# First mixer with its output product in three passes over halves split on GpSimd, input weights laid out by use, areas filled in another order, constants loaded last

## What is computed

```python
def token_mixer(x, w_in, b_in, sinks, ln_v_g, ln_v_b, w_spatial, b_spatial, w_out, b_out):
    proj = x @ w_in + b_in
    q, k, v = proj[..., :o1], proj[..., o1:o2], proj[..., o2:o3]
    u, g = proj[..., o3:o4], proj[..., o4:]
    attn = sliding_window_attention(q, k, v, sinks)
    sgu = chunked_spatial_gating(u, g, ln_v_g, ln_v_b, w_spatial, b_spatial)
    return jnp.concatenate([attn, sgu], axis=-1) @ w_out + b_out

mix = token_mixer(x, ...)
h = layer_norm(DEEPNORM_ALPHA * x + mix, ln1_g, ln1_b)
ffn = routed_experts(h, ...)          # 32 experts, top 4, each 3 x 1024 x 1024 weights
x = layer_norm(DEEPNORM_ALPHA * h + ffn, ln2_g, ln2_b)
```

## Time and profile before

| | us |
|---|---|
| median of 3 runs | 1471.69 |
| lowest, highest | 1471.09, 1472.19 |
| the profiled execution | 1471.71 |
| its span, first to last instruction | 1469.9 |
| TensorE busy | 1393.4 (95%) |
| VectorE busy | 535.1 (36%) |
| ScalarE busy | 342.0 (23%) |
| GpSimd busy | 90.1 (6%) |

### The profile page before, as it was taken

The page is one execution under the profiler, slowest core; times in us unless marked ns, Lnnn a source line. Parts: engine busy times, 40 slices in busy tenths (PEclk is TensorE's granted clock), DMA queues, the critical chain, the costliest instruction groups (busy, mean ns, idle before and its releaser), DMA issues.

```text
span 1469.9 us, 23417 instructions
## 1 busy us (share of the span) xinstructions
PE 1393.4 (95%) x10106; PEld 788.4 (54%) x10106; DVE 535.1 (36%) x980; ACT 342.0 (23%) x504; POOL 90.1 (6%) x44
## 2 busy tenths in 40 slices
PE   8999999999998999899898999999999999999998
PEld 6553333333333333333333333333979989899997
DVE  1772111211211211121112111213989658777766
ACT  0531000100100110010001000102765543444442
POOL 0000000000000000000000000002000050122232
PEclk9999999999999999999999999999999999999999
DMA  9799999999999999999999999998544114255552
GB/s 363 267 401 396 428 428 428 435 432 431 428 433 433 431 430 430 431 433 430 429 426 436 432 427 434 433 427 364 181 144 144 75 44 159 89 198 185 189 182 86
DMA packets 34469, 491.36 MB, mean 334 GB/s; under 512 B 3825, under 2 KB 4337, under 8 KB 12305
## 3 DMA queue, kind: packets, MB, share of 16 engines
q1 hardware_dynamic: 34272, 490.47, 80.5%
q10 hardware_dynamic: 144, 0.13, 0.0%
HBM read 489.54 MB, written 1.05 MB: 334 GB/s over the span
## 4 chain that ended last, share of the span: by engine, by line
PE 67%; DMA 28%; DVE 2%; ACT 1%; issue 0%; POOL 0%; SPq 0%; DVEq 0%; ACTq 0%
DMA ring<-in_w_exp 18%; PE bank L891 17%; DMA work<-in_w_exp 10%; PE bank L920 9%; PE bank L948 8%; PE bank L949 8%; PE bank L950 8%; PE bank L844 2%; PE bank L832 2%; PE bank L703 2%; PE bank L755 2%; PE bank L673 1%; ACT spare L1537 1%; PE bank L852 1%; PE bank L911 1%; PE bank L906 0%
## 5 line engine op out<-in xcount | busy, mean ns | idle before, releaser
L891 PE MATMUL bank<-ring,spare 128*64 128x512 f32 x1344 | 300.6, 600 | 24.0 <-DMA ring<-in_w_exp 23.8
L2066 DVE TENSOR_SCALAR work<-bank 128x512 f32<-128x512 f32 x32 | 22.1, 691 | 739.7 <-PE bank L891 739.7
L891 PEld LDWEIGHTS bank<-ring,spare 128*64 128x64 f32 x1344 | 98.4, 138 | 214.8 <-issue 184.3
L920 PE MATMUL bank<-ring,spare 128*64 128x512 f32 x672 | 148.8, 595 | 14.7 <-ACT spare L1537 14.7
L949 PE MATMUL bank<-work_parts,ring_parts 128*128 128x256 f32 x568 | 159.4, 281 | 0.0
L1533 ACT ACTIVATE work<-work 128x512 f32<-128x512 f32 x32 | 20.2, 631 | 534.5 <-DVE work L2066 534.5
L891 PE MATMUL bank<-work,spare 128*64 128x512 f32 x576 | 128.0, 593 | 8.4 <-DMA work<-in_w_exp 8.4
L949 PEld LDWEIGHTS bank<-work_parts,ring_parts 128*128 128x128 f32 x568 | 107.8, 190 | 1.1
L920 PEld LDWEIGHTS bank<-ring,spare 128*64 128x64 f32 x672 | 46.9, 137 | 103.1 <-issue 90.3
L948 PE MATMUL bank<-hn_hi,ring_parts 128*128 128x256 f32 x352 | 99.4, 282 | 0.0
L950 PE MATMUL bank<-hn_hi,ring_parts 128*128 128x256 f32 x352 | 99.1, 282 | 0.0
(11 more groups left out here) (467 smaller groups left out, 1977.4 us busy)
## 6 DMA issues: line engine op xcount, KB each, us to landing
ring<-in_w_exp SPq DMA_DIRECT2D x57, 4096.0 KB, 31.5
work<-in_w_exp SPq DMA_DIRECT2D x17, 4096.0 KB, 31.6
work<-in_w_exp SPq DMA_DIRECT2D x20, 2048.0 KB, 28.1
spare<-in_w_exp SPq DMA_DIRECT2D x12, 2048.0 KB, 28.3
ring<-in_w_exp SPq DMA_DIRECT2D x12, 2048.0 KB, 24.3
ring<-in_ffn_up SPq DMA_DIRECT2D x22, 1024.0 KB, 4.8
ring<-in_ffn_down SPq DMA_DIRECT2D x22, 512.0 KB, 3.4
ring<-in_w_in SPq DMA_DIRECT2D x2, 2048.0 KB, 17.4
```

Of the source, the lines that this page charges most:

```text
L891: ins = pe.matmul(to[n2 * CAP:(n2 + 1) * CAP, :], x_e[:, 4 * j + 2 * half + kk, :], w[:, b, kk, n2 * BANK:(n2 + 1) * BANK], start=False, s ...
L920: ins = pe.matmul(y_bank[n2 * CAP:(n2 + 1) * CAP, :], hidT[:, k % 4, k // 4 * CAP:(k // 4 + 1) * CAP], w[:, kk, n2 * BANK:(n2 + 1) * BANK] ...
```

## The change

**Output product.** `three_passes` moves ahead and `project_out` uses it. w_out is split on GpSimd, one k-tile at a time: a cast to an upper half (`w_out_hi`: k 0 to 3 in `spare`, 4 and 5 where the probabilities were, 6 and 7 where xT was) and a subtraction that leaves the rest in the place of w_out (`w_out_lo`). ScalarE writes the upper half of the mixer's output (`mix_hi`, four k-tiles, used twice), VectorE the rest (`mix_lo`). The last k-tile of the attention part for the second tokens comes behind the transposes of the gate.

**Areas.** w_in arrives as three arrays, `w_qkv`, `w_g`, `w_u`, each contiguous for a partition; w_g and w_u lie in the two halves of area 1, xT in the place of the rows that are loaded late. Area 0 is filled from `proj_done` 2 on, half 0 of area 1 from 4, half 1 from 6, APART's first half from `mix_first` on. The second block's constants come last.

**LoRA.** The last 32 columns of the gate LoRA stand twice, so that the two K=32 steps use different rows.

The diff, cut to its core:

```diff
-        xT = ring[:, 14336:16384].rearrange("p (k t) -> p k t", k=KD)
-        w_in = ring[:, 0:KD * 1792].rearrange("p (k n) -> p k n", k=KD)
-        w_out = ring[:, 16384:24576].rearrange("p (k n) -> p k n", k=KD)
+        w_qkv = ring[:, 0:KD * W_QKV].rearrange("p (k n) -> p k n", k=KD)
+        w_g, w_u = (ring[:, (2 + n) * SLOT:(3 + n) * SLOT].rearrange("p (k n) -> p k n", k=KD) for n in range(2))
+        w_out, w_out_lo = (a[:, 2 * BLOCK:3 * BLOCK].rearrange("p (k n) -> p k n", k=KD) for a in (ring, ring_parts))
+        late_rows_at = rows_at["ln2_g"][0]
+        xT = rows_sb[:, late_rows_at:late_rows_at + KD * T].rearrange("p (k t) -> p k t", k=KD)
...
+        w_out_hi = [spare_parts[:, k * D:(k + 1) * D] for k in range(4)]
+        for name, at in (("out_hi_a", prob_at), ("out_hi_b", rows_sb_at + late_rows_at)):
+            two = alias(name, work_base, at, 2 * D)
+            w_out_hi += [two[:, n * D:(n + 1) * D] for n in range(2)]
+        mix_hi = alias("mix_hi", work_base, prob_at + 2 * D, D).rearrange("p (k t) -> p k t", k=4)
...
+        mix_lo = work_parts[:, mixT_at:mixT_at + KD * T].rearrange("p (k t) -> p k t", k=KD)
...
-            sp.dma_start(w_in[:, :, W_QKV + G1:], A["w_in"][:, :, W_QKV + G1:]).then_inc(w_g_in, 16)
+            sp.dma_start(w_g, A["w_g"]).then_inc(w_g_in, 16)
             sp.dma_start(wsT, A["wsT"]).then_inc(w_u_wsT_in, 16)
-            sp.dma_start(w_in[:, :, W_QKV:W_QKV + G1], A["w_in"][:, :, W_QKV:W_QKV + G1]).then_inc(w_u_wsT_in, 16)
+            sp.dma_start(w_u, A["w_u"]).then_inc(w_u_wsT_in, 16)
...
-            first_half(APART, 0)
+            sp.wait_ge(proj_done, 2)
+            for half in range(2):
+                first_half(0, half)
+            sp.wait_ge(proj_done, 4)
+            first_half(1, 0)
             sp.wait_ge(attn_done, 1)
             sp.dma_start(bias_all[0:BIAS_ROWS, :], A["bias"]).then_inc(bias_in, 16)
             sp.wait_ge(proj_done, 6)
-            for half in range(2):
-                first_half(0, half)
-            for half in range(2):
-                first_half(1, half)
+            first_half(1, 1)
             sp.wait_ge(mixed_done, 1)
             sp.wait_ge(ug_biased, 4)
             first_half(3, 0)
             sp.wait_ge(mix_first, 1)
             first_half(2, 0)
+            first_half(APART, 0)
             sp.wait_ge(mix_done, 4)
             first_half(2, 1)
             sp.wait_ge(h_ready, 2)
             first_half(APART, 1)
-            sp.wait_ge(router_done, 2)
+            sp.wait_ge(third_part, 2)
+            sp.wait_ge(router_done, 3)
+            first_half(3, 1)
...
+            def three_passes(to, left, right, start, stop):
+                pe.matmul(to, left[0], right[0], start=start, stop=False, skip_group_check=True)
+                pe.matmul(to, left[0], right[1], start=False, stop=False, skip_group_check=True)
+                return pe.matmul(to, left[1], right[0], start=False, stop=stop, skip_group_check=True)
             def project_out(t, ks):
+                rows = slice(t * P, (t + 1) * P)
                 for n in range(2):
+                    cols = slice(n * BANK, (n + 1) * BANK)
                     for k in ks:
-                        ins = pe.matmul(bank[mix_bank[t][n]][:, :], mixT[:, k, t * P:(t + 1) * P], w_out[:, k, n * BANK:(n + 1) * BANK],
-                                        start=k == 0, stop=k == KD - 1)
+                        ins = three_passes(bank[mix_bank[t][n]][:, :], (mix_hi[:, k % 4, rows], mix_lo[:, k, rows]),
+                                           (w_out_hi[k][:, cols], w_out_lo[:, k, cols]), k == 0, k == KD - 1)
                     if ks[-1] == KD - 1:
                         ins.then_inc(mix_done, 1)
                 return ins
-            pe.wait_ge(attn_ready, 2)
-            pe.wait_ge(w_out_in, 4 * 16)
+            pe.wait_ge(mix_ready, 2)
+            pe.wait_ge(out_split, 2 * 4)
             pe.wait_ge(ug_biased, 4)
             project_out(0, range(0, 4))
-            project_out(1, range(0, 4)).then_inc(mix_first, 1)
+            project_out(1, range(0, 3))
...
-            pe.wait_ge(sguT_ready, 1)
+            project_out(1, range(3, 4)).then_inc(mix_first, 1)
+            pe.wait_ge(out_split, 2 * KD)
+            pe.wait_ge(mix_ready, 3)
             project_out(0, range(4, 6))
-            pe.wait_ge(sguT_ready, 2)
+            pe.wait_ge(mix_ready, 4)
             project_out(0, range(6, KD))
             project_out(1, range(4, KD))
...
-                ins = pe.matmul(bank[2 + t][:, :], lora[0:CH, 2, t * P:(t + 1) * P], w_gate_up[0:CH, 1, :], start=False, stop=True)
+            for t in range(TT):
+                rows = slice(t * CH, (t + 1) * CH)
+                ins = pe.matmul(bank[2 + t][:, :], lora[rows, 2, t * P:(t + 1) * P], w_gate_up[rows, 1, :], start=False, stop=True)
...
-                act.copy(mixT[:, 2 * b:2 * b + 2, :], bank[3 + b][:, :].rearrange("p (k t) -> p k t", k=2)).then_inc(attn_ready, 1)
+                act.copy(mix_hi[:, 2 * b:2 * b + 2, :], bank[3 + b][:, :].rearrange("p (k t) -> p k t", k=2)).then_inc(attn_ready, 1)
...
+            act.wait_ge(mix_first, 1)
+            for b in range(2):
+                act.wait_ge(sguT_done, b + 1)
+                act.copy(mix_hi[:, 2 * b:2 * b + 2, :], bank[(2, 7)[b]][:, :].rearrange("p (k t) -> p k t", k=2)).then_inc(attn_ready, 1)
...
             def first_part(t):
                 act.wait_ge(h_ready, t + 1)
+                act.wait_ge(mix_done, 2 * TT)
                 act.copy(h_part[:, 0, t, :], h[:, t, :]).then_inc(split_ready, 1)
...
+            def mix_rest(n, of):
+                dve.wait_ge(attn_ready, n + 1)
+                return dve.tensor_tensor(mix_lo[:, 2 * n:2 * n + 2, :], of[:, :].rearrange("p (k t) -> p k t", k=2),
+                                         mix_hi[:, 2 * (n % 2):2 * (n % 2) + 2, :].bitcast(F32), ALU.subtract)
+            for b in range(2):
+                mix_rest(b, bank[3 + b]).then_inc(mix_ready, 1)
...
-                dve.wait_ge(sguT_done, b + 1)
-                dve.tensor_copy(mixT[:, 4 + 2 * b:6 + 2 * b, :], bank[(2, 7)[b]][:, :].rearrange("p (k t) -> p k t", k=2)).then_inc(sguT_ready, 1)
+                mix_rest(2 + b, bank[(2, 7)[b]]).then_inc(mix_ready, 1)
...
+            pool.wait_ge(w_out_in, 4 * 16)
+            for k in range(KD):
+                if k == 4:
+                    pool.wait_ge(pT_done, 3)
+                if k == 6:
+                    pool.wait_ge(proj_done, 6)
+                pool.tensor_copy(w_out_hi[k], w_out[:, k, :]).then_inc(out_split, 1)
+                pool.wait_ge(out_split, 2 * k + 1)
+                pool.tensor_tensor(w_out_lo[:, k, :], w_out[:, k, :], w_out_hi[k].bitcast(F32), ALU.subtract).then_inc(out_split, 1)
```

78 lines of the change are left out of this document (37 added, 41 removed).

## The result

| | before | after |
|---|---|---|
| median, us | 1471.39 (4 runs) | 1483.41 (4 runs) |
| lowest, highest | 1468.65, 1472.19 | 1482.24, 1484.70 |
| profiled execution's span | 1469.9 | 1481.4 |

The changed kernel is slower: ratio 1.0081, 95% interval 1.0069 to 1.0093, +12.0 us where 1483.0 was forecast.

What follows compares the result with a forecast made beforehand. Bound taken: the first expert matmul's start, set by the first mixer, plus a constant expert stage. Terms 0 + 8.9 + 1.7 + 1.5 + 0.3 - 1.1 = +11.3 us on 1471.7 gave 1483.0 us, range 1474 to 1488.

Steps and rivals of the forecast that it cites:

- What bounds the kernel: Expert stage: its end is the first expert matmul's start (111.98 us) plus a constant; earlier loads cannot help.
- fill order: Weight areas 0 and 1 filled from 28 us on, ending the dry stretch: 0 us.
- The constants' +0.3: Second block's constants, queued behind the last half area, may push the first expert refill: +0.3 us, bounds 0 and +1.5.
- Output product: First mixer: three passes save 5.8 us, all spent waiting for the bias chain ahead of ScalarE's copies; net +0.1 us.
- The split on GpSimd: First mixer: GpSimd's casts and subtractions hold VectorE's two-SBUF-input instructions; third bias cast at 93.5, not 84.55; product +8.9 us.
- rival (a): First mixer: only subtractions hold VectorE, or small instructions slip in; +2.6 to +6.6 in place of 8.9, chance 0.19.
- Cold TensorE: Output product's second part: lower clock after a wait of some 8 us, +1.7 us, bounds 0 and 3.4.
- Behind the product: After the output product: ScalarE's first part of h waits, GpSimd's later subtraction delays VectorE: +1.5 us, bounds +0.5 and +2.
- LoRA: Gate LoRA: two K=32 steps on different array rows can run side by side: -1.1 us, bounds -1.1 and 0.

Runs made afterwards that it cites:

- Run 2: Changed kernel with ScalarE's third bias cast and VectorE's second bias subtraction behind the gated branch's halves, GpSimd's split unchanged: 1476.93 us, ratio 1.0043.
- run 4: Changed kernel plus twelve idle full-precision matmuls of 128x512 in the wait ahead of the output product's second part: 1488.32 us, ratio 1.0125.
- runs 3 and 7: Changed kernel, casts on ScalarE, third bias cast late: 3 without w_out's lower half, 1469.29 us; 7 with it, subtracted by GpSimd and VectorE, 1467.32 us.
- run 1: Changed kernel with ScalarE casting w_out's upper halves in place of GpSimd, no subtraction, lower half left out, still 96 passes: 1475.48 us, ratio 1.0030.
- the kernel before, moved: Kernel before plus sixteen idle full-precision 32x32 matmuls in TensorE's wait at about 28 us, moving its program by 32 weight loads: 1472.90 us, ratio 1.0015.
- the changed kernel, moved back: Changed kernel plus 48 idle 32x32 matmuls at the start, putting TensorE's program back to the position of the kernel before: 1481.69 us, ratio 1.0069.

## Why the prediction was right, and where not

**What bounds the kernel**: as said. The stage from the first expert to its end is a constant, 898.3 us against 898.5 (and within 0.4 us in twelve profiles), and layout, fill order and late constants are worth nothing. The constants' +0.3 was not there, and w_out landed at 42.73, not at 41.4: the windows moved more bytes a second, 420 against 389, without bringing it forward.

**Output product**: right. ScalarE's copies stand behind the third bias cast, and the 5.8 us are spent on waiting. Run 2 against run 4 shows it by order alone, runs 3 and 7 show the gain where the chain is out of the way.

**The split on GpSimd**: right in mechanism and size. Forecast for the third cast's end 93.5 instead of 84.55, measured 94.60 in the profiled run and between 92.8 and 94.7 in the three other runs that have this order and this split. That casts hold too, on which rival (a) turned, the row of 43.12 answers. The Trainium skill's rule of the exclusive lock ("SBUF — State Buffer", section "SBUF: two separate sides") agrees with these rows. The Trainium skill's other rule, 6 us for a first call ("GPSIMD Engine Reference", section "Instruction dispatch"), does not: GpSimd's first subtraction started at 43.90, 0.07 behind the cast.

**Cold TensorE**: forecast +1.7 within 0 to 3.4. The second part took 12.5 us in place of 11.0, +1.5; run 1 shows 2.9, run 4 none. The prediction took waits of 2.1 to 2.3 us for today's longest and left out the 5.60 us at the program's start, behind which ten matmuls of 128x256 took 4.05 us where the next such ten took 2.32.

**Behind the product**: forecast +1.5; from the product's end to the experts 16.57 us against 15.22, +1.35.

**LoRA**: forecast -1.1; measured -1.24 in the rows.

**What was missing** is a term: the program's position. I had put the 32 more matmuls down as time on TensorE only. The medians size it at 0.0015 x 1471 = 2.2 us (the kernel before, moved) and at 0.0012 x 1471 = 1.8 (the changed kernel, moved back), both with intervals of some 1.5 us; the rows at 2.2 and 2.6. In the profiled execution the changed kernel is 12.98 us late at the experts, 12.8 at the last down product, and 14.2 where the last stage begins (1288.21 and 1302.42 us), in spite of the LoRA gain; at the end it is 11.5, because this execution's last stage was a short one and that of before a long one.

So the agreement of 1483.0 with 1483.4 is partly luck. The main term was right, at the product's end 11.6 us late where 8.9 + 1.7 = 10.6 was forecast. One term of some 2.3 us was missing, and without the short last stage the profiled run would have ended 14 us late. What brings the medians to 12.0 is not shown: they mix both kinds of last stage, and the turns of GpSimd and VectorE do not always fall as badly as in the profiled run (the third cast at 92.8 in one).

## What to carry to other kernels

Idle time of GpSimd is no free place while VectorE is on the critical path: either move what GpSimd does to where VectorE works on PSUM or waits, or do half of it on ScalarE. Cutting it into small pieces turns the loss round: VectorE is then free and GpSimd starves. A faster matmul form is worth what the queue ahead of its operands lets through, so look first at what stands ahead of the copies that feed it. And when an edit adds instructions to an engine, compare the stops without a named cause far behind it, before the edit is judged by a few us.

## What the runs showed that I had not expected

TensorE stood still at fixed loads of its program, for up to 3.3 us, each time until 1.2 to 1.6 us after a packet of instructions had landed. Sixteen idle matmuls cost 3.5 us by the ratios, and 48 gained 1.6 (3.4 between the two profiled executions, 0.7 of it ahead of the experts). Behind waits of 2.39 and 2.77 us the clock fell as behind one of 6.8. At the program's start the first ten matmuls took 4.63 us and behind idle ones 2.43, while the clock column has 1.00 for both.
